# Second block's mixer scores: one full-precision product replaced by three products of rounded halves and rests

## The chip, the cores and the metric

The kernel runs on one core of one Trainium2 chip. The metric is the device time of one execution in microseconds (us). Three runs of the kernel before stand beside each other below, and one execution was taken with the hardware profiler.

## The reference, cut to what matters

Two transformer blocks run one after the other on 512 tokens of width 1024, in float32. The second block puts 16 meta tokens ahead of the 512 (528 rows), runs a feed-forward layer, then a token mixer, then another feed-forward layer. The mixer has three branches (A2, B2 and C2 in the program), which share one input projection:

```
# A2: 4 heads x 2 maps of 64, all keys; the two maps' softmaxes are subtracted
s = einsum("bqhmd,bkhmd->bhmqk", qb, k) * scale + t5_bias
a = softmax(s)[:, :, 0] - lam * softmax(s)[:, :, 1]
# B2: 8 heads of 64, keys of the grid's neighbourhood + 16 meta keys
s = where(col_ok, einsum(q_row, k_nb) * scale + bias, NEG);  sm = einsum(q_row, km) * scale
# C2: 8 query heads, 2 key heads of 64, band of 128 + 16 meta keys, sink in the softmax
s_b = where(valid, einsum(qb, kb) * scale + band_bias, NEG);  s_m = einsum(qb, km) * scale + bias
merged = sum_i sigmoid(xn @ w_gate[i]) * (y_i @ w_branch[i]);  return merged @ w_out
```

The change is in how those `einsum` scores of queries against keys are made.

## The kernel before, in words

A phase list runs through the first block ("front"), its feed-forward, then the second block: feed-forward, "mixers", output projection, feed-forward, end. All activations are held with features on the 128 partitions and tokens along the free axis, so that `acc` and `sco` (four PSUM banks of 512 floats each) take products [feature, token] or [query, key]. The large products are already made in three passes of rounded operands: each weight tile and each activation is split into a half rounded to fp32r (`w_hi`, `xn_hi`) and the rest (`w_lo`, `xn_lo`), and PE adds hi·hi, hi·lo and lo·hi (line 1474 in the mixers). ACT makes the halves (line 1710), DVE the rests (line 2272).

In the mixers phase the order of all work is a list, `ORDER`, made by `work_of_mixers` and walked by every engine with its own part. Its entries are: `dense` (some of the 8 tiles of a projection; `ITEMS` names them k, q, v, kv, gate, branch), `pair` (the scores of one tile of 128 queries for two heads or two maps; 48 of them, 32 in A2 and B2, 16 in C2), `turn` (transposes of probabilities, plus a small transpose of the 16 meta columns into `meta_turned`, in bank 1 of `sco`), `vturn` (transposes of values), `value` and `both` (probabilities by values), `oturn` (transposes of the outputs of an A2 head after DVE has scaled them). Each of the twelve turns (three branches, four heads or head pairs) needs its own q and v, and k once per turn (kv once per two turns in C2).

When a k item is done, ACT copies it to `kbuf` (line 1960) and frees the accumulator; a q item goes to `qbuf` (line 1964); a v item to `vT`. DVE has nothing to do for these items. The v item that follows q is "wide" (528 columns, two banks), so that PE waits for both accumulator slots before it. The scores (line 1509, `scores`) of a pair are products of 64 partitions each: the first head's features lie on partitions 0 to 63 of `qbuf` and `kbuf`, the second's on 64 to 127. For A2 and B2 a pair is four full-precision products: 16 meta keys and 512 keys of the first head, 512 and 16 of the second. Because bank 1 is shared with `meta_turned`, the pair waits for `meta_out`, which DVE raises after it copied the last turned meta columns (`take_meta`, lines 2632 and 2634). DVE then adds bias and finds maxima (`score`, lines 2593 to 2604), ACT takes exponentials (line 1990), DVE normalizes and mixes (`mix_maps`, lines 2611 to 2619). At the end of a head of A2, DVE scales the outputs (`take_low`, lines 2682 and 2685), and PE's `oturn` (line 1598) waits for that (`o_scaled`).

Each engine works through its own list strictly in order:

```
for what, j, *part in ORDER:
    if what == "dense" and part[1] == ITEMS[j][3]:
        if later is not None:
            split_item(later)
        take_item(j)
        later = j
```

So what ACT or DVE does in `take_item` comes before its part of the next `turn`, `value` or `oturn`, and the split of the next weights comes after that.

Of the kernel before, what the change touches and what calls it, by code (L numbers as in the profile page):

```python
# [23 lines left out]
P = 128  # L24
D = 1024
SEQ = 512
# [426 lines left out]
def unit_of_value(v):  # L453
# [9 lines left out]
                                          e[0] == "turn" and (e[1] < 16 or e[1] % 2 == 0))}  # L463
TURN_LIST = list(TURNED)


# [70 lines left out]
def events(phase):  # L537
# [14 lines left out]
    if kind == "mixers":  # L552
        e = items(len(ITEMS[0::2]), len(ITEMS[1::2]))
        count = {name: sum(x[0] == name for x in ORDER) for name in ("pair", "turn", "value", "vturn", "oturn")}
        gates, branches = (sum(x[0] == kind for x in ITEMS) for kind in ("gate", "branch"))
        e.update(s_full=count["pair"], meta_scored=32, scored=UNITS, negm=UNITS, probs=UNITS, lam_step=16, mixed=32,
                 pt_full=len(TURNED), pt_a=len(TURNED), meta_full=len(META_TURNED),
# [91 lines left out]
def build(nc, A, out):  # L649
    with ExitStack() as ctx:  # L650
# [15 lines left out]
        w_lo = [sb(f"w_lo{s}", [P, HALF, P], F32R) for s in range(2)]  # L666
        qbuf = sb("qbuf", [P, 2, T])
        kbuf = sb("kbuf", [P, 2, T])
        vT = sb("vT", [P, T])
# [36 lines left out]
        def meta_of(v):  # L706
# [50 lines left out]
        turned_of = [acc[:, 2, :], sco[:, 3, :]]  # L757
        meta_turned = sco[0:META, 1, 32:32 + 2 * P]
        score_of = [sco[:, 0:2, :].rearrange("p a b -> p (a b)")[:, 0:T],
                    sco[:, 1:3, :].rearrange("p a b -> p (a b)")[:, SEQ - META:2 * SEQ]]  # L760
# [392 lines left out]
        def _(pe):  # L1153
# [295 lines left out]
            def mixers():  # L1449
# [32 lines left out]
                def scores(pair):  # L1482

                    name, i, t, _ = place_of_unit(2 * pair)
                    counts["pairs"] += 1
                    if name != "C2":
                        pe.wait_ge(S["meta_out"], n.at("meta_out", counts["meta"]))
                    if pair == 0:
                        pe.wait_ge(S["root_ready"], n.at("root_ready", 0))
                    if t == 1:  # L1490

                        for kind in ("kv" if name == "C2" else "k", "q"):
                            j = ITEMS.index((kind, name, i // 2 * 2 if kind == "kv" else i, KT))
                            pe.wait_ge(S[f"acc_free{j % 2}"], n.at(f"acc_free{j % 2}", k_of_item(j)))
                    pe.wait_ge(S["scored"], n.at("scored", 2 * pair))
                    if name == "C2":
# [5 lines left out]
                        parts = [(hh, 2 * hh, to, c, keys) for to, c, keys in parts for hh in range(2)]  # L1502
                    else:
                        parts = [(0, 1, 0, 0, META), (0, 0, 0, META, SEQ), (1, 2, 0, META, SEQ), (1, 1, SEQ - META, 0, META)]
                    for x, (hh, bank, to, c, size) in enumerate(parts):
                        r = slice(64 * hh, 64 * hh + 64)
                        if name != "C2" and x == 3:
                            pe.wait_ge(S["meta_scored"], n.at("meta_scored", pair + 1))
                        mm = pe.matmul(sco[:, bank, to:to + size], qbuf[r, i % 2, TILES[t][0]:TILES[t][0] + P],  # L1509
                                       kbuf[r, keys_at(name, i), c:c + size], start=True, stop=True)  # L1510
                        if name != "C2" and x == 0:
                            mm.then_inc(S["meta_scored"], 1)
                    mm.then_inc(S["s_full"], 1)
# [188 lines left out]
        def _(act):  # L1702
# [247 lines left out]
            def mixers(following):  # L1950

                def take_item(j):
# [4 lines left out]
                    if kind != "branch":  # L1957
                        act.wait_ge(S[f"item_done{slot}"], n.at(f"item_done{slot}", k))
                    if kind == "k":
                        act.activation(span(kbuf[:, at % 2, :], 2), banks(acc, 0, 2), ACT.Copy).then_inc(free, 1)  # L1960
                    elif kind == "v":
                        act.activation(span(vT[:, :], 2), banks(acc, 0, 2), ACT.Copy).then_inc(free, 1)
                    elif kind == "q":
                        act.activation(qbuf[:, at % 2, META:T], acc[:, slot, :], ACT.Copy).then_inc(free, 1)
                    elif kind == "kv":
                        for half in range(2):
                            act.activation(span(kbuf[64 * half:64 * half + 64, at // 2, :], 2),
                                           banks(acc, 0, 2, slice(0, 64)), ACT.Copy)
                        act.activation(span(vT[0:64, :], 2), banks(acc, 0, 2, slice(64, P)), ACT.Copy).then_inc(free, 1)
                    elif kind == "gate":  # L1970
                        if name == "B2":
# [238 lines left out]
        def _(dve):  # L2210
# [340 lines left out]
            def mixers(following):  # L2551
# [139 lines left out]

                dve.wait_ge(S["meta_zero"], n.at("meta_zero", 1))
                later = None
                for what, j, *part in ORDER:
# [210 lines left out]
```

## Time and profile before

| | us |
|---|---|
| median of 3 runs | 2276.01 |
| lowest, highest | 2275.7, 2278.1 |
| span of the profiled execution | 2277.5 |
| PE busy in it | 2219.2 (97%) |
| DVE, ACT busy | 1243.9 (55%), 903.5 (40%) |

The list of runs does not mark which execution was profiled; its span is 1.5 us above the median and 0.6 us below the highest run. A busy PE here means that some matmul was in flight: matmuls overlap, so the start of one to the start of the next, in the timeline, tells what one costs, and not its own duration. In the trace every full-precision product appears as two records of the same shape, and the rounded ones as one.

### The profile page before, as it was taken

To read this page: it belongs to the slowest core of one execution; us is meant where nothing else is said; L and a number is where in the kernel's file an instruction comes from. 1 tells how busy PE (TensorE), PEld (TensorE's weight loads), DVE (VectorE), ACT (ScalarE), POOL (GpSimd) and SP (SyncE) were. 2 spreads that over 40 slices of the span, in tenths; PEclk is the share of its full clock that TensorE was granted. 3 is DMA by queue.
4 is the path that set the end of the run, shared out by engine and by line. 5 is a ranking of instruction groups with operands and counts; after the bars stand their busy time and mean duration, and the time that the engine had idled before them with its cause. 6 is when DMAs were issued, how large, how long until landed. Compare 5 with 4: busy or idle time off the path is not lost.

```text
span 2277.5 us, 36049 instructions
## 1 busy us (share of the span) xinstructions
PE 2219.2 (97%) x12592; PEld 1820.2 (80%) x12592; DVE 1243.9 (55%) x2668; ACT 903.5 (40%) x1815; POOL 220.5 (10%) x201
## 2 busy tenths in 40 slices
PE   8999999999999999999999899999999999999998
PEld 6567766778888889999999777777777787888887
DVE  5779786467736745533442545544555655443442
ACT  5455445444414443322322444444444433322332
POOL 0100043310000031000001000111100130000001
PEclk9999999999999999999999999999999999999999
DMA  4111211235533342342233222243333233332332
GB/s 119 36 37 37 65 47 52 79 102 150 157 102 95 113 129 78 91 129 88 85 106 99 57 85 81 74 111 94 98 92 98 81 97 89 95 108 77 97 105 75
DMA packets 400393, 205.67 MB, mean 90 GB/s; under 512 B 68956, under 2 KB 393928, under 8 KB 400284
## 3 DMA queue, kind: packets, MB, share of 16 engines
q1 hardware_dynamic: 399365, 203.83, 31.3%
q8 instruction: 63, 1.03, 0.2%
q10 hardware_dynamic: 919, 0.43, 0.1%
q14 instruction: 46, 0.38, 0.1%
HBM read 201.94 MB, written 14.80 MB: 95 GB/s over the span
## 4 chain that ended last, share of the span: by engine, by line
PE 64%; issue 19%; DVE 4%; ACT 2%; POOL 1%; POOLq 0%; DVEq 0%; ACTq 0%
PE acc L1169 34%; PE acc L1474 16%; PE acc L1220 5%; PE sco L1509 2%; PE acc L1573 1%; PE acc L1569 1%; DVE w_lo L2272 1%; PE sco L1262 1%; PE sco L1549 1%; POOL vT L1095 1%; PE acc L1309 1%; PE acc L1549 0%; PE sco L1529 0%; PE acc L1296 0%; DVE bias L2260 0%
## 5 line engine op out<-in xcount | busy, mean ns | idle before, releaser
L1710 ACT ACTIVATE w_hi<-raw 128x512 fp32r<-128x512 f32 (+4 forms) x656 | 372.0, 614 | 694.4 <-PE acc L1169 661.2
L2272 DVE TENSOR_TENSOR w_lo<-raw,w_hi 128x512 fp32r<-128x512 f32 (+4 forms) x656 | 423.2, 685 | 143.8 <-ACT w_hi L1710 139.5
L1169 PE MATMUL acc<-xn_hi,w_hi 128*128 128x512 f32 (+1 forms) x1408 | 421.1, 340 | 2.1 <-DVE qbuf L2826 2.1
L1169 PE MATMUL acc<-xn_lo,w_hi 128*128 128x512 f32 (+1 forms) x1408 | 422.1, 340 | 0.0
L1169 PE MATMUL acc<-xn_hi,w_lo 128*128 128x512 f32 (+1 forms) x1408 | 420.3, 339 | 0.0
L1169 PEld LDWEIGHTS acc<-xn_hi,w_hi 128*128 128x128 f32 x1408 | 241.9, 188 | 35.8 <-DVE qbuf L2826 3.0
L1169 PEld LDWEIGHTS acc<-xn_lo,w_hi 128*128 128x128 f32 x1408 | 241.2, 188 | 31.2 <-issue 0.5
L1169 PEld LDWEIGHTS acc<-xn_hi,w_lo 128*128 128x128 f32 x1408 | 241.5, 188 | 30.0
L1169 PE MATMUL acc<-hid_lo,w_hi 128*128 128x512 f32 (+1 forms) x832 | 261.5, 349 | 0.0
L1169 PE MATMUL acc<-hid_hi,w_lo 128*128 128x512 f32 (+1 forms) x832 | 260.6, 348 | 0.0
L1169 PE MATMUL acc<-hid_hi,w_hi 128*128 128x512 f32 (+1 forms) x832 | 259.8, 347 | 0.8 <-DVE hid_lo L2768 0.8
L2826 DVE TENSOR_TENSOR qbuf<-acc,v_tok 128x512 f32<-128x512 f32 (+1 forms) x132 | 91.7, 695 | 249.8 <-PE acc L1169 249.7
L1474 PE MATMUL acc<-xn_hi,w_hi 128*128 128x264 f32 (+1 forms) x576 | 187.7, 367 | 13.2 <-DVE xn_lo L2299 3.8
L2778 DVE SCALAR_TENSOR_TENSOR h<-acc,h 128x512 f32 (+3 forms) x64 | 44.5, 695 | 267.6 <-PE acc L1169 267.6
L1474 PE MATMUL acc<-xn_hi,w_lo 128*128 128x264 f32 (+1 forms) x576 | 172.8, 341 | 0.0
L1474 PE MATMUL acc<-xn_lo,w_hi 128*128 128x264 f32 (+1 forms) x576 | 172.5, 340 | 0.0
L1169 PEld LDWEIGHTS acc<-hid_hi,w_hi 128*128 128x128 f32 x832 | 144.5, 188 | 23.2 <-issue 1.1
L1169 PEld LDWEIGHTS acc<-hid_lo,w_hi 128*128 128x128 f32 x832 | 144.5, 188 | 21.2
L1169 PEld LDWEIGHTS acc<-hid_hi,w_lo 128*128 128x128 f32 x832 | 144.8, 188 | 20.4
L1474 PEld LDWEIGHTS acc<-xn_hi,w_hi 128*128 128x128 f32 x576 | 98.7, 189 | 36.8 <-issue 17.8
L1220 PE MATMUL acc<-xn_hi,w_hi 128*128 128x512 f32 x240 | 118.6, 494 | 0.9 <-DVE w_lo L2272 0.6
L1474 PEld LDWEIGHTS acc<-xn_hi,w_lo 128*128 128x128 f32 x576 | 99.3, 189 | 12.6
(397 smaller groups left out, 3065.7 us busy)
## 6 DMA issues: line engine op xcount, KB each, us to landing
raw<-in_w_ffn_in SPq DMA_DIRECT2D x176, 256.0 KB, 3.0
raw<-in_w_in SPq DMA_DIRECT2D x118, 256.0 KB, 3.2
raw<-in_w_up SPq DMA_DIRECT2D x88, 256.0 KB, 3.0
raw<-in_w_ffn_out SPq DMA_DIRECT2D x32, 384.0 KB, 3.3
raw<-in_w_gate SPq DMA_DIRECT2D x48, 256.0 KB, 3.0
raw<-in_w_ffn_out SPq DMA_DIRECT2D x32, 320.0 KB, 3.7
raw<-in_w_out SPq DMA_DIRECT2D x32, 256.0 KB, 2.8
bias<-grids_dram SPq DMA_DIRECT2D x64, 128.0 KB, 2.9
```

What stands on the lines that cost most here:

```text
L1095: ins = pool.tensor_tensor(square_sum[:, c0:T], square_sum[:, c0:T], probs[:, s, c0:T], ALU.add)
L1169: mm = pe.matmul(acc[0:m, 2 * slot + b, 0:size], w[slot][:, t, 0:m], x[:, place(t), c:c + size], start=(t == 0 and w is w_hi and x is xh), ...
L1220: mm = pe.matmul(acc[0:m, slot, 0:SEQ], w[slot][:, t, 0:m], x[:, t, META:T], start=(t == 0 and w is w_hi and x is xh), stop=(t == tiles - ...
L1262: mm = pe.matmul(sco[:, hh, :], queries_a[i][r, P * (t - 1):P * t], kbuf[r, i // 2, META:T], start=True, stop=True)
L1309: mm = pe.matmul(acc[64 * hh:64 * hh + 64, 3, o:o + P], front_values(u)[:, 1 + b, 0:64], pt[:, hh, 1 + b, :], start=b == 0, stop=b == 3)
L1474: mm = pe.matmul(acc[:, b if wide else slot, 0:size], w[slot][:, t, :], x[:, t, c:c + size], start=(t == 0 and w is w_hi and x is xh), sto ...
L1509: mm = pe.matmul(sco[:, bank, to:to + size], qbuf[r, i % 2, TILES[t][0]:TILES[t][0] + P], kbuf[r, keys_at(name, i), c:c + size], start=Tru ...
L1549: mm = pe.transpose(turned_of[x % 2][:, b * P:(b + 1) * P], prob_of[u % 4][:, real + b * P:real + (b + 1) * P], eye)
L1710: act.activation(w_hi[slot][:, a:b, :], raw[slot][:, a:b, :], ACT.Copy).then_inc(S[f"hi_ready{slot}"], parts)
L2272: dve.tensor_tensor(w_lo[slot][:, a:b, :], raw[slot][:, a:b, :], w_hi[slot][:, a:b, :].bitcast(F32), ALU.subtract).then_inc(S[f"split{slot ...
L2778: dve.scalar_tensor_tensor(out=x, in0=banks(acc, 2 * s, blk), scalar=factor, in1=x, op0=ALU.mult, op1=ALU.add).then_inc(S[f"acc_free{s}"], 1)
L2826: dve.tensor_tensor(span(scaled[s], blk), banks(acc, 2 * s, blk), span(rstd, blk), ALU.mult).then_inc(S[f"acc_free{s}"], 1)
```

## The change

- Keys: ACT copies the raw k (or kv) item to a new buffer `k_raw`, which frees the accumulator, then waits for its own copy, writes the rounded half `k_hi` and, for A2 and B2, two small pieces `near_hi` of the 16 meta keys (64 x 16 each). DVE writes the rests: two pieces `near_lo`, then `k_lo`.
- Queries: ACT writes the rounded half `q_hi`; DVE takes the rest `q_lo` from the accumulator, and now DVE frees the accumulator.
- Meta keys of a pair of A2 and B2: `near_*` holds both heads' meta keys as a block-diagonal operand (columns 0 to 15 nonzero on partitions 0 to 63, columns 16 to 31 on 64 to 127; DVE zeroes the other blocks once), so that one product over 128 partitions gives both heads' 16 columns, which are written to both ends of bank 1. Three passes make three such products. The inner wait `meta_scored` goes.
- Other keys: three passes for each head, the heads taking turns.
- The new buffers take SBUF room; the scratch reserved for dynamic DMA is set to 1024 bytes. The kernel issues its DMAs from SP and ACT alone.

```
                     if t == 1:
-                        for kind in ("kv" if name == "C2" else "k", "q"):
-                            j = ITEMS.index((kind, name, i // 2 * 2 if kind == "kv" else i, KT))
-                            pe.wait_ge(S[f"acc_free{j % 2}"], n.at(f"acc_free{j % 2}", k_of_item(j)))
+                        keys = ITEMS.index(("kv", name, i // 2 * 2, KT) if name == "C2" else ("k", name, i, KT))
+                        pe.wait_ge(S["key_low"], n.at("key_low", KEY_ITEMS.index(keys) + 1))
+                        j = ITEMS.index(("q", name, i, KT))
+                        pe.wait_ge(S[f"acc_free{j % 2}"], n.at(f"acc_free{j % 2}", k_of_item(j)))
...
                     else:
-                        parts = [(0, 1, 0, 0, META), (0, 0, 0, META, SEQ), (1, 2, 0, META, SEQ), (1, 1, SEQ - META, 0, META)]
-                    for x, (hh, bank, to, c, size) in enumerate(parts):
-                        r = slice(64 * hh, 64 * hh + 64)
...
-                        mm = pe.matmul(sco[:, bank, to:to + size], qbuf[r, i % 2, TILES[t][0]:TILES[t][0] + P],
-                                       kbuf[r, keys_at(name, i), c:c + size], start=True, stop=True)
+                        parts = [(0, META, SEQ)]
+                        for q, near in ((q_hi, near_hi), (q_hi, near_lo), (q_lo, near_hi)):
+                            pe.matmul(meta_scores, q[:, i % 2, queries],
+                                      near[:, at, :].rearrange("p (a b) -> p a b", a=2),
+                                      start=near is near_hi and q is q_hi, stop=q is q_lo)
+                    for to, c, size in parts:
+                        for q, k in ((q_hi, k_hi), (q_hi, k_lo), (q_lo, k_hi)):
+                            for hh in range(2):
+                                r = slice(64 * hh, 64 * hh + 64)
+                                mm = pe.matmul(sco[:, 2 * hh, to:to + size], q[r, i % 2, queries], k[r, at, c:c + size],
+                                               start=k is k_hi and q is q_hi, stop=q is q_lo)
...
                     if kind == "k":
-                        act.activation(span(kbuf[:, at % 2, :], 2), banks(acc, 0, 2), ACT.Copy).then_inc(free, 1)
+                        act.activation(span(k_raw[:, :], 2), banks(acc, 0, 2), ACT.Copy).then_inc(free, 1)
+                        act.wait_ge(free, n.at(f"acc_free{slot}", k))
+                        act.activation(k_hi[:, at % 2, :], k_raw[:, :], ACT.Copy)
+                        for hh in range(2):
+                            r, own = slice(64 * hh, 64 * hh + 64), slice(META * hh, META * hh + META)
+                            last = act.activation(near_hi[r, at % 2, own], k_raw[r, 0:META], ACT.Copy)
+                        last.then_inc(S["key_hi"], 1)
...
                     elif kind == "q":
-                        act.activation(qbuf[:, at % 2, META:T], acc[:, slot, :], ACT.Copy).then_inc(free, 1)
+                        act.activation(q_hi[:, at % 2, META:T], acc[:, slot, :], ACT.Copy).then_inc(S["query_hi"], 1)
...
-                    if kind == "branch":
+                    if kind == "q":
+                        dve.wait_ge(S["query_hi"], n.at("query_hi", QUERY_ITEMS.index(j) + 1))
+                        dve.tensor_tensor(q_lo[:, at % 2, META:T], acc[:, slot, :], q_hi[:, at % 2, META:T].bitcast(F32),
+                                          ALU.subtract).then_inc(S[f"acc_free{slot}"], 1)
+                    elif kind in ("k", "kv"):
+                        s = keys_at(name, at)
+                        dve.wait_ge(S["key_hi"], n.at("key_hi", KEY_ITEMS.index(j) + 1))
...
+                        dve.tensor_tensor(k_lo[:, s, :], k_raw[:, :], k_hi[:, s, :].bitcast(F32), ALU.subtract).then_inc(
+                            S["key_low"], 1)
```

**Where instructions stand.** First PE at a pair of A2 (pair 7). Before:

```order
L1474 MATMUL acc<-xn_hi,w_lo 128x512
L1509 MATMUL sco<-kbuf,qbuf 128x16 [waits scored,meta_out]
L1509 MATMUL sco<-kbuf,qbuf 128x512 x2
L1509 MATMUL sco<-kbuf,qbuf 128x16 [waits meta_scored]
L1474 MATMUL acc<-xn_hi,w_hi 128x512
```

Now (the shapes are those of the output, so that the 64 partitions of the operands do not show):

```order
L1484 MATMUL acc<-xn_hi,w_lo 128x512
L1517 MATMUL sco<-near_hi,q_hi 128x2x16 [waits scored,meta_out]
L1517 MATMUL sco<-near_lo,q_hi 128x2x16
L1517 MATMUL sco<-near_hi,q_lo 128x2x16
L1524 MATMUL sco<-k_hi,q_hi 128x512 x2
L1524 MATMUL sco<-k_lo,q_hi 128x512 x2
L1524 MATMUL sco<-k_hi,q_lo 128x512 x2
L1484 MATMUL acc<-xn_hi,w_hi 128x512
```

Four products (eight records) became nine; three of them span all 128 partitions.

Then ACT after the k item of A2's third head, as the change has it; before, line 1960 stood alone between the `stats` row and the `pt` row:

```order
L2049 ACTIVATE stats<-stats,small 128x4 [waits squares_in]
L1976 ACTIVATE k_raw<-acc 128x528 [waits key_low,item_done0]
L1978 ACTIVATE k_hi<-k_raw 128x528 [waits acc_free0]
L1981 ACTIVATE near_hi<-k_raw 64x16 x2
L2028 ACTIVATE pt<-sco 128x512 [waits o_full,pt_full]
```

Three activations stand between the raw copy and the copy of the turned probabilities.

Last DVE from the same k item on (with `...` for the scores and mixing that stand between, as before):

```order
L2657 SCALAR_TENSOR_TENSOR aux<-aux,stats 128x16
L2593 TENSOR_TENSOR near_lo<-k_raw,near_hi 64x16 [waits key_hi]
L2593 TENSOR_TENSOR near_lo<-k_raw,near_hi 64x16
L2595 TENSOR_TENSOR k_lo<-k_raw,k_hi 128x528
L2670 COPY pt<-sco 16x128 [waits o_full,meta_full]
L2296 TENSOR_TENSOR w_lo<-raw,w_hi 128x512 [waits hi_ready0] x2
...
L2657 SCALAR_TENSOR_TENSOR probs<-probs,stats 128x16
L2585 TENSOR_TENSOR q_lo<-acc,q_hi 128x512 [waits query_hi]
L2720 RECIPROCAL stats<-stats 128x4 [waits o_root]
L2723 TENSOR_SCALAR aux<-aux,stats 128x128 [waits o_rstd]
```

The meta copy (`pt<-sco 16x128`, which raises `meta_out`) now stands behind the key rests, and the scaling that `oturn` waits for stands behind `q_lo`.

## Rows read from the trace of the kernel before

**Rows 1.** The page: busy times, granted clock by 40 slices, chain that ended last.
```profile
PE 2219.2 (97%) x12592; PEld 1820.2 (80%) x12592; DVE 1243.9 (55%) x2668; ACT 903.5 (40%) x1815; POOL 220.5 (10%) x201
...
PEclk9999999999999999999999999999999999999999
...
PE 64%; issue 19%; DVE 4%; ACT 2%; POOL 1%; POOLq 0%; DVEq 0%; ACTq 0%
```
**Rows 2.** Windows: stretch, length, busy PE, PEld, DVE, ACT, POOL, clock, DMA; the mixers.
```profile
1263.00:1823.00 560.00, 527.40 (x3387) 421.73 (x3388) 291.17 (x938) 246.50 (x597) 50.55 (x76) 1.00 0.33 88
```
**Rows 3.** Timeline of PE around pair 7: start us, duration us, engine, line.
```profile
1350.14 0.40 PE L1474 MATMUL acc<-xn_hi,w_lo 128*128 128x512 f32 x1
1350.47 1.35 PE L1509 MATMUL sco<-kbuf,qbuf 64*128 64x16 f32 x8
...
1352.08 0.39 PE L1474 MATMUL acc<-xn_lo,w_hi 128*128 128x512 f32 x1
...
1353.70 0.40 PE L1474 MATMUL acc<-xn_hi,w_lo 128*128 128x512 f32 x1
```
**Rows 4.** Timeline of PE in the first block: a pair without meta keys.
```profile
288.45 0.40 PE L1220 MATMUL acc<-xn_hi,w_lo 128*128 128x512 f32 x1
288.77 1.13 PE L1262 MATMUL sco<-kbuf,qbuf 64*128 64x512 f32 x4
...
290.17 0.40 PE L1220 MATMUL acc<-xn_lo,w_hi 128*128 128x512 f32 x1
```
**Rows 5.** Timeline of PE in the first block: one full-precision product over 96 partitions.
```profile
127.95 1.02 PE L1250 MATMUL sco<-kbuf,qbuf 96*128 96x512 f32 x2
...
129.05 0.39 PE L1220 MATMUL acc<-xn_lo,w_hi 128*128 128x512 f32 x1
```
**Rows 6.** Timeline of PE around turn 2, five transposes between dense products.
```profile
1310.79 0.40 PE L1474 MATMUL acc<-xn_hi,w_lo 128*128 128x512 f32 x1
...
1311.80 0.40 PE L1474 MATMUL acc<-xn_lo,w_hi 128*128 128x512 f32 x1
```
**Rows 7.** Timeline of PE around two pairs of C2, 33 (400 columns) and 35 (256 and 16).
```profile
1675.70 0.40 PE L1474 MATMUL acc<-hid_hi,w_lo 128*128 128x512 f32 x1
...
1677.23 0.40 PE L1474 MATMUL acc<-xn_lo,w_hi 128*128 128x512 f32 x1
...
1697.76 0.40 PE L1474 MATMUL acc<-hid_hi,w_lo 128*128 128x512 f32 x1
...
1699.19 0.39 PE L1474 MATMUL acc<-xn_lo,w_hi 128*128 128x512 f32 x1
```
**Rows 8.** Timeline where q ends just ahead of pair 4.
```profile
1313.87 0.60 ACT L1964 ACTIVATE qbuf<-acc 128x512 f32<-128x512 f32 x1
...
1314.72 1.32 PE L1509 MATMUL sco<-kbuf,qbuf 64*128 64x16 f32 x8 [0.89 <-ACT qbuf L1964]
```
**Rows 9.** The page, groups: count, then busy us and mean ns of one.
```profile
L2826 DVE TENSOR_TENSOR qbuf<-acc,v_tok 128x512 f32<-128x512 f32 (+1 forms) x132 | 91.7, 695 | 249.8 <-PE acc L1169 249.7
```
**Rows 10.** Timeline of ACT at the k item of A2's third head.
```profile
1347.97 0.30 ACT L2025 ACTIVATE stats<-stats,small 128x4 f32<-128x4 f32 x1
1348.17 0.59 ACT L1960 ACTIVATE kbuf<-acc 128x528 f32<-128x528 f32 x1
1348.66 0.59 ACT L2004 ACTIVATE pt<-sco 128x512 f32<-128x512 f32 x1
```
**Rows 11.** Timeline of DVE behind it, up to the scaling of outputs.
```profile
1352.66 1.29 DVE L2272 TENSOR_TENSOR w_lo<-raw,w_hi 128x512 fp32r<-128x512 f32 x2 [4.31 <-ACT w_hi L1710]
...
1357.59 0.17 DVE L2682 RECIPROCAL stats<-stats 128x4 f32<-128x4 f32 x1
```
**Rows 12.** Timeline of PE: the transposes of outputs behind it.
```profile
1358.73 0.66 PE L1598 MATMUL acc<-const,aux 128*128 128x128 f32 x4 [1.42 <-DVE aux L2685]
```
**Rows 13.** Timeline at B2's last q item: ACT's copy, and PE's start on v.
```profile
1602.64 0.60 ACT L1964 ACTIVATE qbuf<-acc 128x512 f32<-128x512 f32 x1 [0.60 <-PE acc L1474]
...
1603.38 0.49 PE L1474 MATMUL acc<-xn_hi,w_hi 128*128 128x264 f32 x2
```

More of the change, by code:

```diff
@@ L464 @@
 TURN_LIST = list(TURNED)
+KEY_ITEMS = [j for j, x in enumerate(ITEMS) if x[0] in ("k", "kv")]
+QUERY_ITEMS = [j for j, x in enumerate(ITEMS) if x[0] == "q"]
 def meta_event(v):
@@ L555, in events @@
         gates, branches = (sum(x[0] == kind for x in ITEMS) for kind in ("gate", "branch"))
-        e.update(s_full=count["pair"], meta_scored=32, scored=UNITS, negm=UNITS, probs=UNITS, lam_step=16, mixed=32,
+        e.update(s_full=count["pair"], key_hi=len(KEY_ITEMS), key_low=len(KEY_ITEMS),
+                 query_hi=len(QUERY_ITEMS), scored=UNITS, negm=UNITS, probs=UNITS, lam_step=16, mixed=32,
                  pt_full=len(TURNED), pt_a=len(TURNED), meta_full=len(META_TURNED),
@@ L666, in build @@
         w_lo = [sb(f"w_lo{s}", [P, HALF, P], F32R) for s in range(2)]
-        qbuf = sb("qbuf", [P, 2, T])
-        kbuf = sb("kbuf", [P, 2, T])
+        with ExitStack() as plain:
+            qbuf, kbuf = (plain.enter_context(nc.sbuf_tensor(name, [P, 2, T], F32)) for name in ("qbuf", "kbuf"))
+        q_hi, k_hi = (sb(name, [P, 2, T], F32R) for name in ("q_hi", "k_hi"))
+        q_lo = sb("q_lo", [P, 2, T], F32R)
+        k_lo = sb("k_lo", [P, 2, T], F32R)
+        k_raw = sb("k_raw", [P, T])
+        near_hi = sb("near_hi", [P, 2, 2 * META], F32R)
+        near_lo = sb("near_lo", [P, 2, 2 * META], F32R)
         vT = sb("vT", [P, T])
@@ L758, in build @@
         meta_turned = sco[0:META, 1, 32:32 + 2 * P]
+        meta_scores = sco[:, 1, :].rearrange("p (a b) -> p a b", b=META)[:, 0:SEQ // META:SEQ // META - 1, :]
         score_of = [sco[:, 0:2, :].rearrange("p a b -> p (a b)")[:, 0:T],
@@ L1963, in take_item @@
                     elif kind == "q":
-                        act.activation(qbuf[:, at % 2, META:T], acc[:, slot, :], ACT.Copy).then_inc(free, 1)
+                        act.activation(q_hi[:, at % 2, META:T], acc[:, slot, :], ACT.Copy).then_inc(S["query_hi"], 1)
                     elif kind == "kv":
                         for half in range(2):
-                            act.activation(span(kbuf[64 * half:64 * half + 64, at // 2, :], 2),
+                            act.activation(span(k_raw[64 * half:64 * half + 64, :], 2),
                                            banks(acc, 0, 2, slice(0, 64)), ACT.Copy)
                         act.activation(span(vT[0:64, :], 2), banks(acc, 0, 2, slice(64, P)), ACT.Copy).then_inc(free, 1)
+                        act.wait_ge(free, n.at(f"acc_free{slot}", k))
+                        act.activation(k_hi[:, at // 2, :], k_raw[:, :], ACT.Copy).then_inc(S["key_hi"], 1)
                     elif kind == "gate":
@@ L2558, in take_item @@
                     slot, k = j % 2, k_of_item(j)
-                    if kind == "branch":
+                    if kind == "q":
[5 more added lines that the diff above has]
+                        dve.wait_ge(S["key_hi"], n.at("key_hi", KEY_ITEMS.index(j) + 1))
+                        if kind == "k":
+                            for hh in range(2):
+                                r, own = slice(64 * hh, 64 * hh + 64), slice(META * hh, META * hh + META)
+                                dve.tensor_tensor(near_lo[r, s, own], k_raw[r, 0:META], near_hi[r, s, own].bitcast(F32),
+                                                  ALU.subtract)
+                        dve.tensor_tensor(k_lo[:, s, :], k_raw[:, :], k_hi[:, s, :].bitcast(F32), ALU.subtract).then_inc(
+                            S["key_low"], 1)
+                    elif kind == "branch":
                         sums[0] += 1
@@ L2692, in mixers @@
                 dve.wait_ge(S["meta_zero"], n.at("meta_zero", 1))
+                for near in (near_hi, near_lo):
+                    for hh in range(2):
+                        r, other = slice(64 * hh, 64 * hh + 64), slice(META * (1 - hh), META * (2 - hh))
+                        dve.tensor_scalar(near[r, :, other], ones[r, 0:2 * META].rearrange("p (a b) -> p a b", a=2), 0.0,
+                                          None, ALU.mult)
                 later = None
@@ L2893 @@
     from concourse.bass_utils import run_bass_kernel_spmd
[L2895 removed]
+    nc = bacc.Bacc("TRN2", target_bir_lowering=False, num_devices=1, dynamic_dma_scratch_size=1024)
     square, onehot, band = shape_constants()
```

10 lines of the change are left out of this document (4 added, 6 removed).

## The prediction, made blind

> **What bounds the kernel.** I read the page first. PE is busy for 97% of the span and its clock is granted in full (the 2.4 GHz level) in all 40 slices; the chain that ended last is PE and its issue for 83% [rows 1]. So a microsecond taken from PE is gained if nothing new makes it wait, and a new wait of PE costs its full length. Next the windows: the change touches only the mixers, 560.0 us, in which PE is busy for 527.4 and idle for 32.6, while DVE (291 us) and ACT (247 us) are about half busy [rows 2]. Then timelines, for two questions: what a pair of scores costs PE, and what stands between ACT's or DVE's work and PE at the places where the change adds to it.
>
> **PE, a pair of A2 or B2 before.** Dense products of 512 columns start 0.23 us apart (from 1352.08 to 1353.70 there are seven steps, 1.62 us) [rows 3]. From the last dense start ahead of pair 7 to the second one behind it are 1.94 us; less two steps of 0.23 the pair costs 1.48 us [rows 3]. How it is made up follows from the first block. One full-precision product of 512 columns takes two records: 1.10 less one step of 0.23 is 0.87, so 0.43 each, the time of two passes [rows 5]. A pair of two heads without meta keys costs 1.72 - 0.46 = 1.26 us for four such records [rows 4]. In a row those would take 1.72, so the two heads run side by side, on partitions 0 to 63 and 64 to 127, in 0.86, and the other 0.40 is what going into and out of this half-height use costs. Of it 0.10 is seen directly: the pair starts at 1350.47 instead of at 1350.37 [rows 3]. The meta keys account for the other 0.22 of 1.48.
>
> **PE, the same pair after.** Three passes for each head, side by side, at a dense step each: 3 x 0.23 = 0.70, and the same 0.40. The trace has no rounded product on 64 partitions. From below a pass is a quarter of a full-precision product, 0.215 [rows 5]; from above the heads do not overlap, 0.46 for both. I take 0.23, because the row of the dense products is the same kind of product with the same number of columns. The three meta products over 128 partitions have only 32 columns, and weights of 128 columns ahead of each. Five transposes, which load as many columns, cost 1.01 - 0.46 = 0.55, or 0.11 each [rows 6]; the first load hides beneath the dense product ahead, so I take 2 x 0.11 + 0.01 = 0.23; bounds are 0.03 (loads hidden) and 0.33. Sum 1.33, a **gain of 0.15 us a pair**. With the bounds together it lies between 0.37 gained and 0.64 lost.
>
> The Trainium skill, page "TensorE: Matmul & The Clock Gate", Part 3, The mechanism, says that a weight load overlaps with a matmul in flight only when its row group differs. By that the second and third pass of each head would show its load. The rows speak against it: the second record of each head in the front's pair would then cost more than the 1.26 holds. It is a rival below.
>
> **C2's 16 pairs.** Pair 33, 400 columns, costs 1.53 - 0.46 = 1.07 [rows 7]; after, a pass is 400/512 of 0.215 plus 0.02, 0.19, so 0.40 + 0.56 = 0.96, gain 0.11. Pair 35, with 256 columns and a separate 16, costs 1.43 - 0.46 = 0.97 [rows 7]; after, 0.40 + 3 x 0.13 + 0.23 for three small passes = 1.02, a loss of 0.05. A quarter of the pairs are of each of these kinds, the other two lie between. Middle 0.03 to 0.06; I take **0.9 us** for all.
>
> **How much of it arrives.** Where PE then waits for a chain of ACT and DVE that did not start from that pair, the pair's gain is lost: this holds for 5 of 32 (pairs 2, 7, 11, 15 and 18, the pairs that stand between a k item or a mixing chain and the wait). 27 x 0.15 = 4.0, with C2 **4.9 us gained**.
>
> **New waits of PE.** All of them come from work that ACT and DVE must now do in order.
> - *q straight ahead of its first pair* (pairs 0 and 4). Now ACT's copy ends at 1314.47 and the pair starts 0.25 later, having waited 0.89 [rows 8]. After, DVE takes the rest from PSUM in 0.70 [rows 9] and PE starts some 0.16 behind it: +0.64 each, **1.3**.
> - *The transposes of outputs* (`oturn` 0, 1 and 2). ACT's step from the key copy to the next work is 0.49 [rows 10]. After, `k_hi` adds 0.49 and 0.14 for waiting on its own copy, two near pieces 0.15 each (a 128x4 activation took 0.20 to the next start, [rows 10]; a tenth is the least I would give it): 0.93. Everything ACT does next is late by that, and DVE waited 4.31 us for it (weights, 1352.66), then has no gap up to the scaling at 1357.59 [rows 11]. On top `q_lo` stands ahead of the scaling, a step of 0.62. PE already waits there 1.42 us [rows 12], so it gets both: 1.55, twice; the third time DVE has 0.3 to spare, 1.25. Sum **4.35**. The fourth (`oturn` 3) has a `both` between and pays 0.2.
> - *The meta copy behind `k_lo`.* Pair 7 waits for it until about 1350.9 instead of 1350.47 [rows 3]; this is swallowed by the wait above.
> - *q ahead of a wide v in B2.* ACT's copy ends at 1603.24, PE starts v at 1603.38 [rows 13]. After, DVE frees the slot: +0.65. The same edge one turn earlier lies behind 1.2 us of value products: 0.25. Sum **0.9**.
> - *Nothing* for kv and q of C2 and for turn 2: the next item there does not need the slot, or the mixing ends just as PE comes. Zeroing of the diagonal's other blocks and the smaller DMA scratch cost nothing: DVE does the first while PE runs the first k item, and no DMA of the kernel is of the kind that uses it. If that cover failed, the zeroing would cost 0.4.
>
> Waits: 1.3 + 4.35 + 0.2 + 0.9 = 6.75. **Sum: 6.75 - 4.9 = +1.8 us.** On the profiled execution that is 2277.5 to 2279.3; it lay 1.5 above the median of the runs, so the forecast is 2276.0 + 1.8 = **2277.8 us**. A measurement of this kernel can tell about 0.2%, 4.6 us, from no change, so I forecast none.
>
> **Rivals.**
> - *The loads show* (the rule above). Two loads of 0.11 a pair turn the gain of 0.15 into a loss of 0.07, 1.9 us over 27 pairs, and in C2 0.9 of gain into some 2.6 of loss: 6.75 + 1.9 + 2.6 = +11.3, 2287. For it: a rounded pass is half as long as a full-precision record, so there is less to hide beneath. Against: 0.11 is still under 0.21, and rows 4. Chance 0.10.
> - *ACT and DVE are late at more places* than the seven I count: 8 k items and 12 q items put up to 0.9 and 0.6 into in-order queues. It decides when PE reaches a turn or a split less than about 1 us after DVE finished it; turn 2 is such a place. Ten more such places at 0.6 give +7.8, **2284, slower**. Chance 0.15.
> - *The heads do not overlap* in rounded form. A pair of A2 then costs 0.40 + 6 x 0.23 + 0.23 = 2.01, 0.53 more, 17 us for 32, and C2 some 8 more: with the waits +32, 2308. Against: rows 4 show the overlap in full precision. Chance 0.05.
> - *Only the gain arrives*: DVE and ACT catch up ahead of PE's waits, because those waits are bounded elsewhere (by ACT's square root, or by PE's own values). Then all 32 pairs count: -(4.8 + 0.9) and up to 1.3 of waits back, or passes at 0.215 and hidden meta loads on top: about -6, 2270. Against: rows 11, DVE without a gap. Chance 0.12.
> - The forecast, within a few us of nothing: 0.58.
>
> **Numbers.** Faster by over 0.2% is the gain-only case, with a little of the forecast's lower edge: 0.14. Slower: 0.10 + 0.15 + 0.05, less what of the second case stays under 4.6: 0.28. Same 0.58. The range takes the gain-only case in half, and the loads' case at its top: 2271.5 to 2287.
>
> **What would show it.** A pair from dense to dense, less two steps: 1.33 where it was 1.48; over 1.5 the loads show, near 2.0 the heads do not overlap. Starts of line 1524's records: two within some hundredths of a us, then 0.23. PE's wait ahead of `oturn` 0: about 3 us instead of 1.42, and its releaser still DVE's scaling; that of pairs 0 and 4: 1.5 instead of 0.89, ended by DVE's `q_lo`. PE idle in the mixers: 32.6 + 6.75 + some 0.8 of lost gain, about 40. If PE's busy time in the mixers does not fall by about 5 us, or idle grows by over 12, my terms are wrong.

## The result, and the profile after

The changed kernel takes **2286.11 us** (median of 6 runs, 2282.2 to 2288.3), the kernel before 2277.02 us (6 runs, 2275.7 to 2278.4): ratio 1.0038, 95% interval 1.0027 to 1.0050. That is 9.1 us slower, twice the 0.2% that can be told from no change. I had forecast +1.8 and no change. The profiled execution took 2285.51 us with a span of 2283.7, 6.2 more than the 2277.5 of before. What lies around the span is 1.8 us in nearly every run here, so the profiled execution of before took about 2279.3, 2.3 above its median. The prediction set its span of 2277.5 beside whole times; that slip does not enter its forecast. One further run of the kernel before, 3455.67 us at a granted clock of 0.583, was in the chip's slow state and is left out of every median, mean and ratio here.

The page of the changed kernel, the lines that answer to [rows 1]: PE is 4.1 us less busy in a span 6.2 us longer, and the clock's digits, which round over 57 us each, show nothing.

```profile
PE 2215.1 (97%) x12672; PEld 1824.0 (80%) x12672; DVE 1260.3 (55%) x2710; ACT 913.4 (40%) x1841; POOL 220.0 (10%) x201
PEclk9999999999999999999999999999999999999999
PE 62%; issue 19%; DVE 5%; ACT 3%; POOL 1%; DMA 0%; POOLq 0%; DVEq 0%; ACTq 0%; SPq 0%
```

**The pairs.** The timeline of PE and its weight loads (PEld) around pair 9 of the changed kernel, a pair ahead of which PE does not wait (start, duration, instruction), to be laid beside [rows 3]. A row of line 1524 stands for both heads.

```profile
1377.63 0.39 PE L1484 MATMUL acc<-xn_hi,w_lo 128*128 128x512 f32 x1
1377.86 0.18 PE L1517 MATMUL sco<-near_hi,q_hi 128*128 128x32 f32 x1
1377.89 0.26 PE L1517 MATMUL sco<-near_lo,q_hi 128*128 128x32 f32 x1
1378.00 0.26 PE L1517 MATMUL sco<-near_hi,q_lo 128*128 128x32 f32 x1
1378.19 0.50 PE L1524 MATMUL sco<-k_hi,q_hi 64*128 64x512 f32 x2
...
1378.53 0.40 PE L1524 MATMUL sco<-k_lo,q_hi 64*128 64x512 f32 x2
1378.53 0.19 PEld L1524 LDWEIGHTS sco<-k_hi,q_lo 64*128 64x128 f32 x2
1378.76 0.40 PE L1524 MATMUL sco<-k_hi,q_lo 64*128 64x512 f32 x2
...
1379.42 0.39 PE L1484 MATMUL acc<-xn_lo,w_hi 128*128 128x512 f32 x1
```

From 1377.63 to 1379.42 are 1.79; less two steps of 0.23 the pair costs 1.33, as forecast. The third pass starts 0.23 behind the second, and its two weight loads run beneath the second. Worked out in the same way over the first 28 pairs, the median is 1.335 where it was 1.474. C2's pairs are of four kinds, four of each: 0.86 to 0.77, 1.07 to 0.95, 1.17 to 1.16 and 0.97 to 0.99, together a gain of 0.8. A pair that starts straight behind a wait does not gain: less their waits, pair 0 costs 1.60 (1.53 before) and pairs 7 and 11 some 1.60 (1.48 before).

**The waits.** The view of waits of PE in the mixers of the changed kernel: who waited for whom, total us, times, longest. Under it the same view of the kernel before, its one row that answers to the first.

```profile
PE acc L1611 <- DVE aux L2723: 8.1, 3, 3.2
PE sco L1517 <- DVE q_lo L2585: 3.2, 2, 1.6
PE acc L1484 <- DVE q_lo L2585: 2.2, 3, 1.1
PE sco L1517 <- DVE pt L2670: 1.2, 2, 0.6
```
```profile
PE acc L1598 <- DVE aux L2685: 5.5, 4, 1.8
```

PE waits 2.48, 2.44 and 3.16 us ahead of `oturn` 0, 1 and 2 (1.42 in [rows 12], then 1.44 and 1.77), 1.61 ahead of pairs 0 and 4 (0.89 in [rows 8]), and 0.57 twice for the meta copy behind `k_lo`. The wide v behind q waits 1.11 at the fourth head of A2, where PE waited 0.82 for the scaling before, and 0.26 and 0.85 in B2, where it did not wait. Place by place that is 7.4 us more.

**The clock.** Windows of the changed kernel (columns as in [rows 2]): the mixers, then the stretches around pair 4. Then the one such stretch in the mixers of the kernel before.

```profile
1263.00:1823.00 560.00, 519.59 (x3426) 422.57 (x3424) 306.93 (x976) 255.26 (x618) 48.82 (x75) 0.99 0.33 87
1300.76:1304.17 3.41, 3.41 (x18) 3.41 (x17) 0.18 (x1) 2.03 (x5) 0.00 (x0) 0.50 0.32 85
1304.17:1317.83 13.66, 11.90 (x74) 9.52 (x73) 6.76 (x21) 6.39 (x14) 0.00 (x0) 1.00 0.20 59
1317.83:1321.24 3.41, 3.41 (x18) 3.08 (x15) 1.85 (x8) 0.00 (x0) 0.00 (x0) 0.50 0.09 17
```
```profile
1300.35:1303.76 3.41, 3.41 (x18) 3.17 (x17) 0.00 (x0) 1.66 (x5) 0.00 (x0) 0.50 0.23 70
```

The first of the changed kernel's two stretches and the one of the kernel before stand just behind the same place, an idle stretch of PE at turn 0. The view names no engine that ended it (`issue`). Timelines of PE, changed and before:

```profile
1300.36 0.27 PE L1542 MATMUL sco<-const,aux 128*16 128x128 f32 x1 [1.98 <-issue]
```
```profile
1299.24 0.27 PE L1529 MATMUL sco<-const,aux 128*16 128x128 f32 x1 [1.95 <-issue]
```

The changed kernel's second stretch is new: behind pair 4's longer wait the granted clock is at 1.2 instead of 2.4 GHz for 3.41 us, which the kernel before does not show there. The timeline of PE says what that costs: a wide step of two records of 264 columns goes from 0.25 us to 0.44.

```profile
1316.73 0.26 PE L1517 MATMUL sco<-near_hi,q_hi 128*128 128x32 f32 x1 [1.61 <-DVE q_lo L2585]
1318.76 0.64 PE L1484 MATMUL acc<-xn_lo,w_hi 128*128 128x264 f32 x2
1319.20 0.64 PE L1484 MATMUL acc<-xn_hi,w_lo 128*128 128x264 f32 x2
1321.34 0.41 PE L1484 MATMUL acc<-xn_lo,w_hi 128*128 128x264 f32 x2
1321.59 0.40 PE L1484 MATMUL acc<-xn_hi,w_lo 128*128 128x264 f32 x2
```

A stretch of 3.41 us at half clock does at least the work of 1.7, so it costs at most 1.7 us. Three profiles of the changed kernel (two more are in the table below) put it at 1.6: from two to five such stretches the mixers grow by 4.7 us, 0.46 for each us at half clock. Counting half of the time at half clock gives the one number that can be compared between profiles: the mixers **at full clock**, from their first product to the last start of a dense one, less half of the time at half clock. Before: 582.9 - 3.4/2 = 581.2. After: 588.3 - 6.8/2 = 584.9, 3.7 more. The mean granted clock of a whole run (each run lists it) was 0.9937 on average over the six runs of the changed kernel, and 0.9961 over 66 runs of the kernel before that the experiments below brought. The difference of 0.0024 is 5.5 us of 2284. 3.7 and 5.5 are 9.2, for 9.1 measured. Over all 17 runs of the changed kernel, the repeats below included, the mean clock is 0.9940, which is 4.9 us; with the 3.7 that is 8.6, for 7.5 to 9.1 measured. So the working theory (A below): at full clock the waits outweigh what the pairs gain by some 4 us, and the waits then bring the clock down, which costs as much again or more.

### The profile page after: what moved, and what is told of

Same layout as the page of the kernel before. It is cut to its first block, busy times and chain, and to the rows that moved or that the text cites. A ratio compares the mean times of both kernels' runs of the same rounds, so it can differ in the third digit from the quotient of the medians.

```text
span 2283.7 us, 36286 instructions
## 1 busy us (share of the span) xinstructions
PE 2215.1 (97%) x12672; PEld 1824.0 (80%) x12672; DVE 1260.3 (55%) x2710; ACT 913.4 (40%) x1841; POOL 220.0 (10%) x201
## 4 chain that ended last, share of the span: by engine, by line
PE 62%; issue 19%; DVE 5%; ACT 3%; POOL 1%; DMA 0%; POOLq 0%; DVEq 0%; ACTq 0%; SPq 0%
PE acc L1179 34%; PE acc L1484 15%; PE acc L1230 5%; PE sco L1524 2%; PE acc L1586 1%; DVE w_lo L2296 1%; PE acc L1582 1%; PE sco L1272 1%; POOL vT L1105 1%; PE acc L1319 1%; PE sco L1562 1%; PE acc L1562 0%; ACT w_hi L1723 0%; PE sco L1542 0%; PE acc L1306 0%
```

## The experiments

Twelve runs. The columns: median us; ratio to the kernel before on the same chip, with its interval; then of the profiled execution, in us: the mixers' length, in it time at half clock, the length at full clock, PE's idle time (length less busy, from the windows); and the mean granted clock over all runs of the kernel.

| kernel | us | ratio | mixers | half | full | idle | clock |
|---|---|---|---|---|---|---|---|
| before | 2277.02 | | 582.9 | 3.4 | 581.2 | 31.7 | 0.996 |
| changed | 2286.11 | 1.0038 | 588.3 | 6.8 | 584.9 | 39.5 | 0.994 |
| changed, e2 | 2284.56 | 1.0038 (1.0025-1.0051) | 589.9 | 10.2 | 584.8 | 39.6 | 0.994 |
| changed, e9 | 2284.25 | 1.0038 (1.0026-1.0051) | 593.0 | 17.1 | 584.4 | 39.6 | 0.994 |
| e1 passes | 2273.61 | 0.9980 (0.9971-0.9989) | 577.1 | 0.0 | 577.1 | 32.3 | 0.996 |
| e5 waits | 2284.45 | 1.0036 (1.0024-1.0048) | 593.7 | 10.2 | 588.6 | 39.4 | 0.996 |
| e3 hold, both | 2279.76 | 1.0013 (1.0004-1.0022) | 587.0 | 3.4 | 585.3 | 29.7 | 0.996 |
| e10 hold, pairs | 2283.66 | 1.0037 (1.0024-1.0051) | 588.5 | 6.8 | 585.1 | 37.3 | 0.995 |
| e11 hold, outputs | 2282.02 | 1.0027 (1.0015-1.0039) | 589.8 | 10.2 | 584.7 | 32.2 | 0.996 |
| e4 early | 2279.11 | 1.0014 (1.0006-1.0023) | 586.6 | 10.2 | 581.5 | 36.5 | 0.995 |
| e7 early, q raw | 2275.04 | 0.9992 (0.9983-1.0000) | 581.6 | 10.2 | 576.5 | 31.0 | 0.995 |
| e8 all | 2268.41 | 0.9966 (0.9953-0.9979) | 574.9 | 3.4 | 573.2 | 26.9 | 0.996 |
| e6 before, early | 2269.72 | 0.9970 (0.9959-0.9980) | 578.3 | 3.4 | 576.6 | 27.3 | 0.997 |
| e12 before, early, hold | 2272.75 | 0.9984 (0.9975-0.9993) | 578.5 | 3.4 | 576.7 | 26.0 | 0.996 |

**e1: TensorE's side alone.**

```diff
-for q, k in ((q_hi, k_hi), (q_hi, k_lo), (q_lo, k_hi)):
+for x in range(3):
     for hh in range(2):
-        mm = pe.matmul(sco[...], q[r, i % 2, queries], k[r, at, c:c + size], ...)
+        mm = pe.matmul(sco[...], q_hi[r, i % 2, queries], k_hi[r, at, c:c + size], ...)
```

> Only TensorE's side of the change: the rounded products in three passes and the meta product, all from the rounded copies alone (the rests and the meta copies are neither made nor used, so the scores are not the reference's); ScalarE and VectorE work as in the kernel before. Theory A (the change gains what its pairs save, and loses it by waits for ScalarE and VectorE): 4 to 6 us under the kernel before, 2271 to 2273, PE idle in the mixers 33 to 34 us, no stretch at half clock near 1318. Rival B (the rounded products cost TensorE as much as the old ones, by weight loads or by pulling the clock down): at or above the kernel before, 2277 or more, with half clock near 1318 as in the changed kernel.

Measured 3.2 us under the kernel before, 0.6 above the expected range. At full clock the mixers are 4.1 shorter, PE's idle is 0.6 longer, and this window of it, the mixers, shows the full clock from end to end:

```profile
1258.90:1836.00 577.10, 544.78 (x3569) 443.29 (x3570) 301.63 (x967) 252.85 (x613) 61.41 (x83) 1.00 0.34 89
```

So the new products are a gain of 4.1, and rival B falls: by themselves, ahead of waits as short as before, they cost no more and leave the mean clock at 0.996.

**e2: the changed kernel, by a slip.** The edit that was to take the scores in full precision fell into code that is never called, so the kernel issued what the changed kernel issues. It is kept as a repeat; what was expected of it holds for e5.

> Only the other side of the change: ScalarE and VectorE make copies, rests and meta pieces as in the changed kernel, and pairs wait for them, but the scores are taken in full precision from the rounded copies, as before (the rests are left out). Theory A: the waits alone, about 7 us of new idle time of PE, and 1.5 to 4 us more where the clock falls to half behind a wait: 8 to 12 over the kernel before, 2285 to 2289, with half clock near 1318. Rival B (the clock falls because the rounded pairs are lighter work): 6 to 7 over, and no half clock near 1318. Rival C (waits matter little, the new products are the loss): within 3 of the kernel before.

Measured 2284.56, mean clock 0.994. In its profile three stretches at half clock stand in the mixers, where the first profile of the changed kernel had two.

**e5: the other side alone.** Copies, rests and waits as changed, and the pairs as before:

```diff
-for q, k in ((q_hi, k_hi), (q_hi, k_lo), (q_lo, k_hi)):
-    ...
+for x, (hh, bank, to, c, size) in enumerate(parts):
+    ...
+    mm = pe.matmul(sco[:, bank, to:to + size], q_hi[r, ...].bitcast(F32),
+                   k_hi[r, ...].bitcast(F32), start=True, stop=True)
```

> Only ScalarE's and VectorE's side of the change and the waits for it; the scores are taken by four full-precision products per pair, as before, from the rounded copies (the rests are left out of them). Theory A (the pairs' gain is 4 at full clock, the waits cost 7 to 8, the rest is half clock): PE idle in the mixers 39 to 41 us, the mixers at full clock about 588.5 (before 581.2, changed 584.9), 2287 to 2291 in all, 10 to 13 over the kernel before. Rival C (waits matter little): under 5 over the kernel before.

Idle 39.4 and 588.6 at full clock, both as expected: the waits cost 7.4. The time, 2284.45, is under the range, and its six runs had a mean clock of 0.996, not 0.994. So here the same waits cost their length, 7.4 us at full clock and 7.9 in the time, and nothing beyond it shows in the mean. That is close to e2's rival B (the clock falls because the rounded pairs are lighter work: 6 to 7 over, no half clock near 1318), and this profile has no half clock at the pairs. With e1 it says that neither the lighter pairs nor the longer waits alone lower the mean clock; the changed kernel has both. Its profile has three half-clock stretches, and all three stand at the output transposes. The timeline of PE at the first of them (the clock is at half from 1358.80 to 1362.21):

```profile
1359.18 1.11 PE L1609 MATMUL acc<-const,aux 128*128 128x128 f32 x4 [2.52 <-DVE aux L2721]
1360.53 0.64 PE L1484 MATMUL acc<-xn_lo,w_hi 128*128 128x264 f32 x2
1360.97 0.64 PE L1484 MATMUL acc<-xn_hi,w_lo 128*128 128x264 f32 x2
1362.51 0.41 PE L1484 MATMUL acc<-xn_hi,w_hi 128*128 128x264 f32 x2
```

**e3, e10, e11: unread products in place of the waits.** Ahead of a wait PE runs products of 128 columns into a bank that is free, so that it is busy until the wait nearly ends:

```diff
+def hold(out, count):
+    for _ in range(count):
+        pe.matmul(out, ones[:, :], eye, start=True, stop=True)
...
+if pair in (0, 4):
+    pe.wait_ge(S["scored"], n.at("scored", 2 * pair))
+    hold(sco[:, 0, 0:P], 6)
...
-pe.wait_ge(S["o_scaled"], n.at("o_scaled", turn + 1))
 x = TURNED["oturn", turn]
 bank_free(x)
+hold(turned_of[x % 2][:, 0:P], (10, 10, 13, 0)[turn])
+pe.wait_ge(S["o_scaled"], n.at("o_scaled", turn + 1))
```

> The changed kernel with products of 128 columns whose result nobody reads, issued while PE would wait: 6 ahead of the q wait of pairs 0 and 4, 10, 10 and 13 ahead of the wait of the output transposes 0, 1 and 2; they end before the waits do, by the trace. Theory A (part of the +9 is the half clock behind those waits): 1.5 to 4 us under the changed kernel, 2282 to 2284.5, and no half clock between 1310 and 1400. Rival D (the clock's half stretches have nothing to do with the waits): same as the changed kernel or up to 1 us more, half clock near 1318 stays.

It took 2279.76, 2.2 us under its range: 4.7 us less than the changed kernel in its repeats (2284.4), though at full clock the mixers are no shorter. The timeline of PE at `oturn` 0 shows the trade, 2.39 us of idle products and 0.20 of wait for 2.48 of wait:

```profile
1357.30 2.39 PE L1495 MATMUL acc<-const,ones 128*128 128x128 f32 x20
1359.89 0.66 PE L1620 MATMUL acc<-const,aux 128*128 128x128 f32 x4 [0.20 <-DVE aux L2732]
```

At full clock that is 585.3 for 584.9; its mean clock is back at 0.996, and from 1302.54 on the mixers run at full clock. This is the evidence for the second half of theory A: rival D, that the clock has nothing to do with the waits, falls. Which waits? e10 has the first edit alone, e11 the second, e9 neither.

> The changed kernel once more, for the spread of its times and granted clocks beside the next two on the same chip: 2284 to 2287, mean clock 0.993 to 0.995, where the kernel before has 0.995 to 0.998.

> The changed kernel with the unread products only ahead of the waits of pairs 0 and 4 (6 each). In the profiles the added half-clock stretches stand around these two pairs (1297 to 1321): if those waits bring them, nearly all of the 6 us that both kinds of unread products gained comes back: 2280 to 2282, mean clock 0.996. If the output transposes' waits bring them, within 1.5 of the changed kernel.

> The changed kernel with the unread products only ahead of the waits of output transposes 0, 1 and 2 (10, 10, 13). If the waits of pairs 0 and 4 bring the half clock: 2283.5 to 2286, within 1.5 of the changed kernel. If those of the output transposes do, 2280 to 2282.

The profile of e9 has five half-clock stretches, each of them just at or behind a wait of PE: of 1.61 (pair 0), 1.97 (turn 0), 1.61 (pair 4), 2.48 and 2.45 us (`oturn` 0 and 1).

```profile
1279.11:1282.52 3.41, 3.41 (x17) 3.41 (x16) 1.82 (x8) 1.66 (x4) 0.00 (x0) 0.50 0.15 20
1296.17:1299.58 3.41, 3.37 (x16) 3.40 (x17) 0.40 (x2) 2.03 (x5) 0.00 (x0) 0.50 0.38 107
1313.24:1316.65 3.41, 3.41 (x16) 2.65 (x15) 1.85 (x8) 0.00 (x0) 0.00 (x0) 0.50 0.02 7
1361.03:1364.44 3.41, 3.41 (x19) 3.33 (x17) 2.23 (x4) 1.07 (x3) 0.00 (x0) 0.50 0.04 6
1408.81:1412.22 3.41, 3.25 (x15) 3.25 (x16) 1.48 (x4) 1.72 (x3) 0.00 (x0) 0.50 0.00 0
```

With products ahead of the pairs only (e10), the half clock stands at the wait of 3.17 us ahead of `oturn` 2 and nowhere else; with products ahead of the outputs only (e11), around the two pairs and turn 0, and nowhere behind. Windows of e10, then of e11:

```profile
1260.00:1450.84 190.84, 169.51 (x1092) 143.01 (x1092) 106.25 (x323) 88.21 (x193) 4.79 (x10) 1.00 0.28 76
1450.84:1457.67 6.83, 6.07 (x28) 6.07 (x29) 2.65 (x7) 1.72 (x3) 1.16 (x2) 0.50 0.12 32
```
```profile
1312.82:1316.23 3.41, 3.41 (x15) 2.67 (x15) 1.70 (x7) 0.00 (x0) 0.00 (x0) 0.50 0.03 7
1316.23:1840.00 523.77, 502.01 (x3325) 408.54 (x3324) 282.35 (x905) 236.01 (x585) 55.27 (x76) 1.00 0.34 89
```

So in the profiles the stretches go from just the places that were covered. In the times neither edit alone brings what both do: 2283.66 and 2282.02 against 2284.25 on that chip, over ranges of 5 to 7 us with 5 or 6 runs each. The mean clocks rise in steps, 0.9942 (e9), 0.9952 (e10), 0.9957 (e11) and 0.9965 with both (e3, on another chip). My expectation that the pairs' waits carry nearly all of it was wrong; the share of each kind is not settled.

**e4: the scaling out of q_lo's way.** VectorE scales a head's rows of output behind the meta copy of the turn that follows the square root, where it has 2.7 us free (in the changed kernel from 1354.4 to 1357.1), and not at the transposes.

```diff
 elif what == "turn":
     ...
+    if j in (5, 9, 13, 17):
+        scale_rows((j - 5) // 4)
```

> The changed kernel with VectorE scaling the output rows of a head right behind the meta copy of the turn after that head's square root, instead of just ahead of the output transposes, where it stood behind q_lo. Theory A: the waits ahead of output transposes 0, 1 and 2 (2.48, 2.44, 3.16 us) fall to at most 0.3 each: 5 to 8 us under the changed kernel, 2278 to 2281. Rival E (those waits are only handed on to the next turn of probabilities, which waits for mixing on the same engine): under 3 us gained, with new waits ahead of turns 6, 10 and 14.

The waits ahead of the transposes are gone, 2279.11, as expected. But part of them was handed on, as rival E had it, only to another place: the wide v right behind needs the slot of q, and `q_lo` frees it behind a mixing. The timeline of PE there, and the row of the waits:

```profile
1358.55 0.60 PE L1611 MATMUL acc<-const,aux 128*128 128x128 f32 x4
1360.28 0.49 PE L1484 MATMUL acc<-xn_hi,w_hi 128*128 128x264 f32 x2 [1.13 <-DVE q_lo L2585]
```
```profile
PE acc L1484 <- DVE q_lo L2585: 7.3, 6, 2.1
```

**e7, e8: the change with its waits taken out.** e7 adds to e4 that ScalarE copies q raw first, as it does the keys, except for the items of pairs 0 and 4. e8 adds three things to e7: the keys' rounded copy and rests behind the next turn; the first 128 queries ahead of the rest for pairs 0 and 4; three unread products ahead of their waits.

```diff
+act.activation(k_raw[:, META:T], acc[:, slot, :], ACT.Copy).then_inc(free, 1)
+act.wait_ge(free, n.at(f"acc_free{slot}", k))
-act.activation(q_hi[:, at % 2, META:T], acc[:, slot, :], ACT.Copy)...
+act.activation(q_hi[:, at % 2, META:T], k_raw[:, META:T], ACT.Copy)...
```
```diff
+act.activation(q_hi[:, at % 2, META:META + P], acc[:, slot, 0:P], ACT.Copy).then_inc(S["first_hi"], 1)
+act.wait_ge(S["first_low"], n.at("first_low", DIRECT.index(j) + 1))
...
 split_hi(j % 2, k_of_item(j) + 1, tiles)
+if ITEMS[j][0] == "k" and j:
+    copy_keys(j)
```

> The changed kernel with the early scaling, and with ScalarE copying q raw first (as it does the keys), which frees the slot, except for the two q items that stand straight ahead of their pair. The waits of the wide v items for q_lo (7.3 us in six places in the run with early scaling alone) go: idle in the mixers 30 to 31 us, 6 to 7 us under early scaling alone: 2272 to 2274, 3 to 5 under the kernel before. Rival (the queues of ScalarE are late by the extra copy of 0.6 us): 2276 or more.

> As the run with q copied raw, and besides: the keys' rounded copy and rests behind the next turn of probabilities (the two waits of 0.57 for the meta copy go), the first tile of queries 128 columns ahead of the rest for pairs 0 and 4 (their waits 1.6 become 0.9 to 1.0), and three products of 128 columns that nobody reads ahead of those two waits. Idle in the mixers 27 to 29 us; 3 us under the run with q copied raw, and at most one half-clock stretch in the mixers: 2268 to 2271. Rival (the moved key work comes late to the pair or the mixing it serves): no gain over the run with q copied raw.

e7: idle 31.0 as expected, 5.0 us less at full clock than e4; with 2275.04, at a mean clock of 0.995, it is 1 us above the range. e8: 2268.41, in its range, **8.1 us faster than the kernel before** and 16 faster than the changed kernel in its repeats, on other chips. Timelines of PE in e8: pair 4 waits 0.23 behind 0.8 us of unread products, and `oturn` 0 for nothing.

```profile
1310.25 0.83 PE L1496 MATMUL sco<-const,ones 128*128 128x128 f32 x6
1311.31 0.25 PE L1531 MATMUL sco<-near_hi,q_hi 128*128 128x32 f32 x1 [0.23 <-DVE q_lo L2632]
...
1353.39 0.60 PE L1625 MATMUL acc<-const,aux 128*128 128x128 f32 x4
1354.33 0.48 PE L1485 MATMUL acc<-xn_hi,w_hi 128*128 128x264 f32 x2 [0.34 <-ACT k_raw L2015]
```

**e6, e12: is it the change that gains this?** The early scaling needs nothing of the change, so the kernel before gets it too, in e12 with the three unread products.

> The kernel before, with VectorE scaling a head's output rows right behind the meta copy of the turn after that head's square root; nothing of the change. The waits of 1.42, 1.44 and 1.77 us ahead of output transposes 0, 1 and 2 go: idle in the mixers 28 us instead of 32.6, 3.5 to 5 us under the kernel before, 2272 to 2273.5, if the slot of q is free by then as it is now. Rival: what PE gains there it waits a little later, for the mixing; under 2 us.

> The kernel before with the early scaling and three unread products of 128 columns ahead of the waits of pairs 0 and 4; nothing of the change. At full clock the mixers take 576.6 as with early scaling alone, against 573.2 in the best version with the change: 2268.5 to 2271. If the change is worth its price once its waits are gone, this stays 1 to 3.5 us above 2268.4; rival: the same within 1 us, for a higher mean clock.

2269.72 and 2272.75. e6 came 2.3 us under its range, with idle 27.3 for 28 expected. Most of what e8 gains comes from the early scaling. At full clock the change is worth 3.4 us in company with it (576.6 to 573.2, all its waits paid); in the times e8 is 1.3 under e6 on the same chip, with runs that lie 3 and 7 us apart, and 4.3 under e12 on another. So a gain is likely, its size open. e12 missed its range by 2 us, and its unread products brought nothing: they are for a wait of 0.89, behind which no profile of the kernel before has the half clock. The one stretch it has in the mixers is behind the idle 1.95 at turn 0, which no kernel here covered.

## Why the prediction was right or wrong

The time lay inside the range, and that was luck: the mechanism forecast a change near nothing, and the 9.1 us came in good part from a cost that it did not have.

- *A pair of A2 or B2, 1.48 to 1.33*: right, 1.474 to 1.335. The loads of the later passes do not show and the heads run side by side, so two rivals fall. The Trainium skill's rule that a weight load overlaps a matmul only of another row group ("TensorE: Matmul & The Clock Gate", Part 3, The mechanism), taken by itself, is not borne out by these rows: the third pass starts 0.23 behind the second in spite of the loads for the same rows.
- *C2, 0.9, and the whole gain of 4.9*: C2 gained 0.8. e1 shows 4.1 at full clock, 0.8 less than forecast. A saving of 0.14 for 0.15 in the other pairs accounts for 0.3 of it, and pairs 0 and 4 for 0.4, since straight behind their wait they cost 1.58 in e1 and 1.53 before. (The bounds given for a pair come out at 0.41 gained and 0.63 lost, not 0.37 and 0.64.)
- *New waits, 6.75*: e5 shows 7.4, and idle time rose by 7.8. By place: pairs 0 and 4 0.72 each for 0.64; `oturn` 0 and 1 1.0 each for 1.55, but the meta copy at pairs 7 and 11, which I let be swallowed, took 0.57 each, which makes the same sum; `oturn` 2 1.4 for 1.25; the fourth head 0.3 for 0.2; q ahead of a wide v in B2 0.26 and 0.85, for 0.9 in all.
- *The sum, +1.8*: at full clock it was +3.7. This much is a matter of sizes: 0.8 less gain, 0.7 more wait.
- *The step that failed* stands in the first paragraph: "its clock is granted in full (the 2.4 GHz level) in all 40 slices", so "a new wait of PE costs its full length". In the changed kernel it cost more; e3 took 4.7 us off by filling the waits alone. I read the clock from the page's digits, which do not show 3.4 us; the kernel before had a stretch of half clock in the mixers, behind its own idle 1.95, and windows would have shown it. The row was there to say that idle time of 2 us can be followed by some 1.6 us of loss, and that five waits were about to grow to 1.6 to 3.2 us. Some three more stretches per run (4.9 to 5.5 us by the mean clocks) are the larger part of the 9.1. No rival had it: the one that ended slower, ACT and DVE late at more places, gave 2284 by ten places that do not exist (idle in the window of [rows 2] is 40.4, and was forecast at about 40).
- The range, 2271.5 to 2287.0, held the time near its upper end, for reasons that it did not contain: its top was there for loads that show, and they do not.

What stays open: with the pairs in full precision and the same waits (e5), the mean clock was 0.996 in six runs, with the rounded pairs 0.994 in 17 runs. So that the waits are needed for the clock's fall is shown (e3), that they suffice is not: whether the lighter pairs take part was not settled, and e5 ran on another chip than e2 and e9.

## What to carry to other kernels

Before a new wait on TensorE is priced at its length, look with windows of a few us behind the waits that are there: where one of that size is followed by half clock, the new one may be too, now and then, and then costs another 1.6 us or so. It was so with the rounded pairs; with pairs in full precision (e5) the mean clock did not fall. Work that is late for a consumer should be sought in the order of the in-order engine that makes it: moving four groups of scalings to where VectorE was idle gained 6.8 us on the kernel before, more than the change of the arithmetic ever did alone (3.2). And a rest that is taken from PSUM keeps a slot; a raw copy first gives it back (in e7 the waits of the wide v for the slot fell from 7.3 to 1.0 us).

## What the runs showed of the hardware

- Every half-clock stretch of the mixers in these profiles stands at or behind idle time of PE of 1.6 us or more, but not all such idle time has one: the changed kernel, with six such places, had 2, 3 and 5 in three profiles of the same program, and e1, with idle 1.97 and 1.77, had none. In those three profiles this makes 4.7 us of difference; the runs of the changed kernel lie between 2281 and 2288.
- Products that nobody reads can save time: 4.7 us for 11 us of them, in e3.
- Rounded products on 64 partitions with their own weights step 0.23, as dense ones on 128 do, two heads at once, and the weight loads between them are hidden. Straight behind a wait a pair of them costs 1.60 us instead of 1.33.
